# One decoder layer on one core: all eight cache pages of a slot issued by SyncE

## The reference

```python
h = rms_norm(x, norm1_g) * (1 + scale1) + shift1          # scale, shift from silu(c) @ w_ada
q_a, k_a, v_a, q_g, k_g, v_g, og_g, gk_lr, gate_a, gate_b = split(h @ w_in)
# A: block-sparse attention, 8 heads of 64, top 3 blocks of 256 keys and the own block
# the 8 sequences read 2048 earlier keys and values each through a page table
k_past = cache_k[layer, pages].reshape(past_len, A_HEADS, A_HEAD_DIM)    # 16 pages of 128 tokens
v_past = cache_v[layer, pages].reshape(past_len, A_HEADS, A_HEAD_DIM)
o_a = attend(q_a, k_a, v_a)
# B: gated linear attention (GLA), 4 heads, chunks of 32, state kept
o_g, s_new = gla_chunked(q_g, k_g, v_g, log_a, s0)
merged = sigmoid(gate_a) * (o_a @ w_branch_a) + sigmoid(gate_b) * (o_g @ w_branch_b)
x = x + gate1 * (merged @ w_out)
# mixture of experts: 4 groups of 8 experts, top 1 group, top 2 experts, SwiGLU, width 512
x = x + gate2 * hier_moe(h2, ...)
```

## Time and profile before

| what | value |
|---|---|
| median of 3 runs | 1489.11 us (1482.4 to 1493.91) |
| span of the profiled execution | 1487.5 us |
| the profiled execution's own time beside it | none is given; the span is used |
| mean granted TensorE clock | 0.955 |
| TensorE busy | 1359.3 us |
| HBM read, written | 355.69 MB, 23.67 MB |

### The profile page before, as it was taken

How to read it: one execution, slowest core, us unless ns; L and a number is a source line. 1 busy time by engine, 2 the same in 40 slices (tenths; PEclk the granted TensorE clock), 3 DMA queues, 4 the chain that set the end, 5 groups by cost and what they waited for, 6 DMA issues and landing times.

```text
span 1487.5 us, 20091 instructions
## 1 busy us (share of the span) xinstructions
PE 1359.3 (91%) x7763; PEld 817.9 (55%) x7763; DVE 329.5 (22%) x824; ACT 292.3 (20%) x595; POOL 225.4 (15%) x308
## 2 busy tenths in 40 slices
PE   6899999899999999999999999799879887888886
PEld 4334687444668677778888777544323333333332
DVE  4233012564332424220000022411110001000114
ACT  3100367442222333210000001301100000000002
POOL 3113333321010201010000011211111111111000
PEclk9999999998999999999999999899998989989998
DMA  9966799977724333233110412899999999999984
GB/s 350 395 249 205 244 348 316 319 286 230 225 57 149 92 118 110 50 86 99 57 57 0 174 50 116 231 395 404 404 405 406 403 403 398 407 394 389 406 348 184
DMA packets 114815, 370.41 MB, mean 249 GB/s; under 512 B 10980, under 2 KB 56309, under 8 KB 95278
## 3 DMA queue, kind: packets, MB, share of 16 engines
q1 hardware_dynamic: 93088, 306.73, 55.0%
q0 software_dynamic: 20384, 59.10, 12.0%
q10 hardware_dynamic: 1262, 3.48, 0.8%
HBM read 355.69 MB, written 23.67 MB: 255 GB/s over the span
## 4 chain that ended last, share of the span: by engine, by line
PE 71%; DMA 22%; DVE 4%; issue 1%; ACT 1%; SPq 1%; POOL 0%; POOLq 0%; ACTq 0%; DVEq 0%
PE ps L1449 64%; DMA ring<-in_w_exp_up 18%; PE ps L1460 7%; DMA ring<-in_w_in 3%; DVE work L1202 1%; DVE work L1438 0%; DVE work L1443 0%; SPq L440 0%; DVE work L1413 0%; DMA work<-h_rows,idx 0%; DMA work<-expert_rows 0%; ACT work L699 0%; SPq L434 0%; DMA expert_rows<-work 0%; DVE stats L1079 0%
## 5 line engine op out<-in xcount | busy, mean ns | idle before, releaser
L1449 PE MATMUL ps<-ring,work 128*64 128x512 f32 (+2 forms) x2720 | 430.6, 506 | 74.5 <-DMA ring<-in_w_exp_up 51.5
L1449 PEld LDWEIGHTS ps<-ring,work 128*64 128x64 f32 (+1 forms) x2720 | 156.5, 131 | 313.6 <-issue 245.8
L1449 PE MATMUL ps<-ring,hx 128*128 128x256 f32 (+3 forms) x880 | 221.3, 444 | 4.5 <-DMA ring<-in_w_in 4.5
L1449 PEld LDWEIGHTS ps<-ring,hx 128*128 128x128 f32 (+1 forms) x880 | 136.3, 175 | 81.1 <-issue 63.6
L1449 PE MATMUL ps<-hx,ring 128*128 128x272 f32 x768 | 179.1, 393 | 0.6 <-DVE work L1202 0.6
L1449 PEld LDWEIGHTS ps<-hx,ring 128*128 128x128 f32 x768 | 145.2, 190 | 31.2 <-DVE work L1202 1.1
L1449 PE MATMUL ps<-work,ring 128*128 128x272 f32 x640 | 151.0, 396 | 0.0
L1449 PEld LDWEIGHTS ps<-work,ring 128*128 128x128 f32 x640 | 122.3, 192 | 26.6 <-issue 1.2
L1449 PE MATMUL ps<-work 32*128 32x256 f32 (+10 forms) x838 | 119.2, 375 | 17.4 <-DVE work L955 7.0
L622 POOL DMA_INDIRECT expert_rows<-work x32 | 32.3, 1010 | 441.5 <-DVE work L1417 430.4
L887 ACT ACTIVATE work<-ps 128x256 f32<-128x256 f32 x32 | 12.3, 384 | 431.2 <-PE ps L1449 431.2
(11 more groups left out here) (289 smaller groups left out, 854.3 us busy)
## 6 DMA issues: line engine op xcount, KB each, us to landing
ring<-in_w_exp_down SPq DMA_DIRECT2D x32, 2048.0 KB, 23.4
ring<-in_w_exp_gate SPq DMA_DIRECT2D x31, 2048.0 KB, 19.5
ring<-in_w_exp_up SPq DMA_DIRECT2D x31, 2048.0 KB, 23.8
ring<-in_w_ada SPq DMA_DIRECT2D x12, 2048.0 KB, 18.6
ring<-in_cache_k SPq DMA_DIRECT2D x64, 256.0 KB, 4.6
ring<-in_cache_k POOLq DMA_DIRECT2D x64, 256.0 KB, 4.9
ring<-in_cache_v SPq DMA_DIRECT2D x64, 256.0 KB, 4.9
ring<-in_cache_v POOLq DMA_DIRECT2D x64, 256.0 KB, 5.2
```

Of the source, the lines that this page charges most:

```text
L1449: return pe.matmul(out, lhsT, rhs, start=start, stop=stop, **k)
```

## The change

The half of the pages that POOL issued goes to SP. `load_pages` has no list of pages and no semaphore array any more; it issues all eight, each counted on the slot's own semaphore, so a block of pages adds 8 x 16 to it instead of 4 x 16. `half_pages`, its calls and the six semaphores `pages{i}_landed` are gone, and `landed` waits once. The order of the blocks, their slots, their use and everything else stay.

```diff
-        page_sem = [sem(f"pages{i}_landed") for i in range(RING)]
...
-                PAGED[(what, i)] = add_block((what, i), PAGES // 4, used)
+                PAGED[(what, i)] = add_block((what, i), 8, used)
...
         def landed(pe, n):
             pe.wait_ge(slot_sem[SLOT_ORDER[n]], stream[n][0])
-            if isinstance(stream[n][1], tuple):
-                paged = [m for m in PAGED.values() if SLOT_ORDER[m] == SLOT_ORDER[n] and m <= n]
-                pe.wait_ge(page_sem[SLOT_ORDER[n]], 16 * PAGES // 4 * len(paged))
...
-        def load_pages(eng, n, pieces, which, sems):
+        def load_pages(eng, n, pieces):
...
-            for q in which:
+            for q in range(8):
...
-                eng.dma_start(slot(n)[:, AW * q:AW * q + AW], src).then_inc(sems[SLOT_ORDER[n]], 16)
+                eng.dma_start(slot(n)[:, AW * q:AW * q + AW], src).then_inc(slot_sem[SLOT_ORDER[n]], 16)
...
-                    load_pages(sp, n, pieces, range(0, 8, 2), slot_sem)
+                    load_pages(sp, n, pieces)
...
-            def half_pages(what, i):
-                n = PAGED[(what, i)]
-                pool.wait_ge(*stream[previous(n)][2])
-                load_pages(pool, n, (what, i), range(1, 8, 2), page_sem)
-
-            pool.wait_ge(s("page_table_in"), 16)
-            for i in range(4):
-                half_pages("k", i)
             pool.wait_ge(s("v_ready"), 5)
...
-            for i in range(4, KEY_PAGES // 8):
-                half_pages("k", i)
-            for i in range(KEY_PAGES // 8):
-                half_pages("v", i)
```

## The result

| | before | changed |
|---|---|---|
| median, us | 1488.14 (1482.40 to 1493.91, 4 runs) | 1534.84 (1531.90 to 1538.93, 4 runs) |
| ratio, 95% interval | | 1.0317 (1.028 to 1.0353) |
| span of the profiled execution, us | 1487.5 | 1530.6 |

The changed kernel is slower by 46.7 us between the medians, by 43.1 us between the profiled spans; 1530 was forecast, from 41.1 us. Each ratio in this document compares the fast executions of the two kernels on one chip, so it can differ a little from the quotient of the medians, and it leaves out three executions in the slower state: one each with fixed pages, with six pages and of the changed kernel repeated. First the page after: busy times, queues, and the engines' shares of the chain that ended last.

What follows compares the result with a forecast made beforehand. TensorE bounds the cache stretch before, SP's page issue after the change. A 39.6 us delay at V15 plus 1.5 for the clock gives 41.1 on 1487.5, 1528.6; the median's 1.6 above the span makes it 1530, range 1518 to 1550.

Steps and rivals of the forecast that it cites:

- What SP pays for a page: SP's issue of cache pages: 1.10 us a page, 9.02 us a slot of eight, against TensorE's 6.0.
- K0 to K3 covered, no slot freed late: K0–K15 are key slots, V0–V15 value slots; K0–K3 land before use, later slots are free in time: no cost.
- Landing: Cache pages land 3.1 us after issue on SP's queue alone, against 4.9 to 5.1 with two queues.
- TensorE's side: TensorE's use of cache pages: K10 first late, V7 33.1 us late, V8 in time, V15 delayed 39.6 us.
- Behind V15: After the last value slot: GLA weights in time by one microsecond, lower clock costs 1.5 us once, the rest moves along.
- No change: Cache page loads: SP's issue counts for little, TensorE stays the bound, 1489 us; chance 0.04.
- Faster: Cache slots: POOL's half lands last and TensorE waits for it, so the change gains 13.2 us, 1476; chance 0.02.
- TensorE's clock: Value stage: idle gaps hold TensorE at 1.2 GHz, so it, not SP, is late at V15; 1537 us; chance 0.10.

Runs made afterwards that it cites:

- fixed pages: Changed kernel with constant page numbers, all eight pages of a slot on SP, no load or check of page numbers: 1485.6 us, ratio 0.9992 to the kernel before.
- six pages: Kernel before with SP issuing six pages of each slot and POOL two (pages 3 and 7): 1486.9 us, ratio 0.9974.
- changed kernel repeated: The changed kernel, unaltered, profiled once more: span 1531.7 us, ratio 1.0311 to the kernel before.
- cheap issue: Changed kernel with one load of eight page numbers a slot, registers of each block's own, no range check: 1489.4 us, ratio 0.9993 to the kernel before.
- seven pages: Kernel before with SP issuing seven pages of each slot and POOL one (page 7): 1507.5 us, ratio 1.0168.

## Why the prediction was right

- *What SP pays for a page.* Right: 1.10 us and 9.02 a slot forecast, 1.10 and 9.11 measured. The 0.09 is one term, the slow pages. I had 0.016 us a page for them; over K5 to V15 the mean distance of two issues was 1.138 us, and K10 and K12 hold a page of over 2 us each. In all the last page left at 419.4, not at 416.6: the largest error of the sum, 2.8 us, 0.4 of it a later K4.
- *K0 to K3 covered, no slot freed late.* Right: SP waited 0.3 us after 165.
- *Landing.* The 3.1 us were right (3.0 in the median; V15's last page took 3.4). The reading behind them was not. I took 4.9 for the price of two queues at once; with cheap issue one queue shows 4.8. What goes with the longer landings is the rate, not the number of queues: from 180 to 240 us one queue landed the keys in 3.0 us at 229 GB/s (changed kernel) and in 4.6 at 339 (cheap issue), two queues in 4.8 and 5.0 at 339 (kernel before).
- *TensorE's side.* The first slot to be late was K9, not K10. The forecast had K9 complete at 221.2; its last page left at 219.0 and took 4.8 us instead of 3.1, and TensorE was ready for it at 220.9. That costs nothing in the end, since SP's chain and not TensorE's sets what follows. K15 came at 278.2 (275.3 forecast), V0 at 291.0 (287 forecast), V7 at 350.7 (347.5), V8 without a wait for its pages at 373.9 (368.8), V15 at 422.8 (419.7). The errors are SP's 2.8 us, the 0.3 of the last landing, and half-speed work inside the stage, which cost nothing at V15. TensorE's 6.0 us a slot is its pace when nothing interrupts it; over K5 to K15 give 6.4 on average, still far under 9.0.
- *Behind V15.* 1.5 us for the lower clock forecast, 9.96 - 8.31 = 1.65 measured; the GLA weights were in time; the rest moved as one piece and was 1.2 us shorter.
- *The rivals.* "No change" falls with the threshold between six and seven pages: the transfers are hidden, the issuing is not. The Trainium skill, "DMA: Bandwidth & Descriptors", section "Issuing engines are not separate DMA queues", is borne out in that the queue on which the pages go makes no difference to their transfer, and in that SP's 1.10 us a page is less than its 3.0 us of landing. It is not borne out as a forecast of the time: landings overlap and issues do not, so here the sequencer's time is the whole difference. "Faster" falls with the last of the cheap versions, which takes all pages from POOL and gains nothing. "TensorE's clock" falls with the repeated profiles, though the margin is a few microseconds: for the last slots TensorE waited 6.2 us in one (V13 to V15) and 5.1 in the other (V14 and V15).
- *What a single profile can give.* 41.1 us stands against 43.1 of the two spans. The parts are V15 3.1 us later than forecast, most of it slow pages, 0.15 more at the lower clock, and 1.2 less behind; so the sum is a little closer than its terms. Against the medians it is 5.6 short; of the other 3.6 us, 2.0 lie in which execution of the changed kernel was profiled, since it took 1532.8 us, 2.0 under its median. The forecast rested on one execution of a kernel in which V15 alone moved by 7.7 us between two profiles.

## What to carry to other kernels

When loads move from one queue to another, count the sequencer's time for each, its register work included, and set what is added over the whole stretch against the time for which the issuing queue waits there. Here 69 us of waits stood against an estimated 62, 94 and 125 us of added issue for six, seven and eight pages (28 slots, 1.116 us a page), which puts the last page no, 25 and 56 us later; it left 1.9 us earlier, 30 and 59 us later. Comparing a slot's issue with the consumer's time for a slot is too strict: six pages took 6.9 us against 6.0 and cost nothing. The bytes did not enter here. If it doesn't fit, the issue can be made cheaper (one load for several numbers, the table in the order of use): here that was as good as a second engine, and no better.

## What the runs showed of the hardware that I had not expected

- A DMA of 64 rows of 2 KB cost SP 477 ns to issue, one of 128 such rows 338 ns: half the transfer, 41% more issue.
- One load of eight consecutive numbers into registers took 524 ns, a load of one 269 ns in the median of the changed kernel. The Trainium skill, "DMA: Bandwidth & Descriptors", section "Latency and other measured facts", gives about 600 ns as the least for such a load; both rows lie below.
- With nothing between them and with constant addresses, DMA instructions took 432 ns in the median (fixed pages); behind register work they took 338. Which of the two differences does it was not tried.
- The kernel before, unchanged, read V15 at 380.1 in one execution and at 387.8 in another, with 14 and 34 us at the lower clock in the value stage.
